# Sink logits as an extra score column, and VectorE's high/low splits spread over the steps of an attention loop

## What is computed

```python
s = jnp.einsum('bqkgd,bskd->bkgqs', qb, kb, preferred_element_type=jnp.float32) * scale
s = jnp.where(mask, s, NEG_INF)
sink = jnp.broadcast_to(sinks.reshape(KV, G)[None, :, :, None, None], s.shape[:-1] + (1,))
p = jax.nn.softmax(jnp.concatenate([s, sink], axis=-1), axis=-1)[..., :-1]
...
return (o * jax.nn.silu(gate)) @ w_out
```

## Time and profile before

| what | value |
|---|---|
| runs | 2717.4, 2725.14, 2715.82 us (median 2717.4) |
| the profiled execution | 2716.97 us, of which the span is 2715.2 us |
| PE busy | 2407.9 us, 89% |
| DVE busy | 1598.5 us, 59% |
| POOL busy | 915.3 us, 34% |
| ACT busy | 765.6 us, 28% |
| mean granted PE clock | 0.921 of full |

### The profile page before, as it was taken

The page is one execution under the profiler, slowest core; times in us unless marked ns, Lnnn a source line. Parts: engine busy times, 40 slices in busy tenths (PEclk is TensorE's granted clock), DMA queues, the critical chain, the costliest instruction groups (busy, mean ns, idle before and its releaser), DMA issues.

```text
span 2715.2 us, 31261 instructions
## 1 busy us (share of the span) xinstructions
PE 2407.9 (89%) x12233; PEld 1833.5 (68%) x12233; DVE 1598.5 (59%) x2435; ACT 765.6 (28%) x1706; POOL 915.3 (34%) x944
## 2 busy tenths in 40 slices
PE   3969898788999899799969989999998997999988
PEld 2756676567987666677747776577677685757666
DVE  7786674763235566664664557674745445958373
ACT  2233202512001355224331233221402215232231
POOL 2873897387800345781120010401302001040030
PEclk6979898798678899899989999999999999999999
DMA  6440455044543100441011211121121121213111
GB/s 213 140 132 8 117 135 129 1 116 117 127 78 62 32 1 3 123 116 63 32 58 59 71 48 63 32 78 63 47 93 63 62 63 33 62 47 93 47 62 62
DMA packets 229157, 200.27 MB, mean 74 GB/s; under 512 B 86835, under 2 KB 213139, under 8 KB 228755
## 3 DMA queue, kind: packets, MB, share of 16 engines
q1 hardware_dynamic: 217491, 156.33, 20.6%
q0 software_dynamic: 11520, 41.95, 5.2%
HBM read 196.16 MB, written 2.10 MB: 73 GB/s over the span
## 4 chain that ended last, share of the span: by engine, by line
PE 57%; POOL 17%; DVE 17%; ACT 5%; issue 3%; DMA 0%; SPq 0%; DVEq 0%; ACTq 0%; POOLq 0%
PE bank L506 13%; PE bank L507 13%; PE bank L508 13%; POOL mix L2220 6%; POOL mix L2217 4%; PE bank L618 4%; DVE wring_parts L1515 3%; PE bank L654 3%; POOL mix L2223 2%; PE bank L632 2%; POOL mix L2204 2%; DVE whi_parts L1514 2%; PE bank L818 2%; DVE qb L1959 1%; PE bank L572 1%
## 5 line engine op out<-in xcount | busy, mean ns | idle before, releaser
L507 PE MATMUL bank<-h_parts,whi_parts 128*128 128x512 f32 (+2 forms) x1336 | 539.5, 404 | 0.0
L1515 DVE TENSOR_TENSOR wring_parts<-wring,whi_parts 128x2048 fp32r<-128x2048 f32 (+1 forms) x138 | 326.4, 2365 | 4.7
L1514 DVE CAST whi_parts<-wring 128x2048 fp32r<-128x2048 f32 (+1 forms) x138 | 192.3, 1394 | 201.5 <-PE bank L508 167.1
L507 PEld LDWEIGHTS bank<-h_parts,whi_parts 128*128 128x128 f32 (+2 forms) x1336 | 253.6, 190 | 69.2 <-issue 5.9
L2220 POOL TENSOR_TENSOR mix<-mix 128x512 f32<-128x512 f32 (+1 forms) x160 | 214.5, 1341 | 12.5
L506 PE MATMUL bank<-vt_parts,whi_parts 128*128 128x512 f32 (+2 forms) x472 | 199.9, 424 | 18.1 <-POOL h_parts L2251 12.1
L507 PE MATMUL bank<-mix_parts,whi_parts 128*128 128x512 f32 x512 | 202.9, 396 | 0.0
L506 PE MATMUL bank<-pt_parts,whi_parts 128*128 128x512 f32 x392 | 166.3, 424 | 36.7 <-DVE wring_parts L1515 20.9
L508 PE MATMUL bank<-vt_parts,wring_parts 128*128 128x512 f32 (+2 forms) x472 | 190.4, 403 | 0.0
L1586 DVE CUSTOM_DVE_ANT_0 bank<-bank,causal 128x128 f32<-128x128 f32 (+3 forms) x256 | 120.2, 512 | 76.0 <-PE bank L618 75.6
L618 PE MATMUL bank<-kb,qb 64*128 64x128 f32 (+3 forms) x1024 | 156.7, 385 | 8.7 <-ACT pr L1199 4.0
(11 more groups left out here) (375 smaller groups left out, 5363.9 us busy)
## 6 DMA issues: line engine op xcount, KB each, us to landing
wring<-in_w_in SPq DMA_DIRECT2D x60, 1024.0 KB, 5.2
mix<-in_ada_w POOLq DMA_DIRECT2D x80, 512.0 KB, 4.6
wring<-in_w_out SPq DMA_DIRECT2D x16, 1024.0 KB, 5.1
wring<-in_mla_w_in SPq DMA_DIRECT2D x10, 1024.0 KB, 7.0
wring<-in_mla_w_out SPq DMA_DIRECT2D x8, 1024.0 KB, 5.2
wring<-in_swa_w_in SPq DMA_DIRECT2D x32, 256.0 KB, 4.7
wring<-in_nsa_w_in SPq DMA_DIRECT2D x32, 256.0 KB, 4.5
wring<-in_nsa_w_in SPq DMA_DIRECT2D x6, 1024.0 KB, 5.2
```

The costliest lines, as they stand in the source:

```text
L507: pe.matmul(bank, lh, rl, start=False, stop=False)
L1514: chain(dve.tensor_copy(high, whole))
L1515: dve.tensor_tensor(low, whole, high.bitcast(F32), ALU.subtract).then_inc(done, 1)
```

## The change

Two edits. First, in L = 1 PE writes the sink of each head as one more column behind the scores, by a matmul of one row of ones (128 columns) with one element of the sink, so that ACT's exponential over n+1 columns sums it too; ACT's 128x1 exponentials and DVE's addition go. Second, `split` is taken apart in the attention loops of all layers: the gate scaling of a unit's output stays at its step, the high cuts follow one step later and the low cuts two steps later; the high cut of a weight unit stays at steps 5 and 9, its low cut moves to steps 7 and 11. In MLA the two high cuts of a unit stand together, and so do the two low cuts. After the last step all three stages follow one another. `prepare` and `split` outside these loops are as before.

```diff
@@ PE, attention, score(m)
+                    if L == 1:
+                        for s in range(2):
+                            row, e = slice(s * HD, s * HD + 1), sink_of(u, s)
+                            pe.matmul(b[s][:, n:n + 1], ones[row, :], sink[row, e:e + 1], start=True, stop=True)
@@ ACT, attention, exps(m)
-                        if L == 1:
-                            e = sink_of(u, s)
-                            act.activation(stat_at(3, m, s), sink[:, e:e + 1], ACT.Exp, scale=-1.0, bias=stat_at(0, m, s))
-                        act.activation(rows_slot(m, s)[:, 0:n], bank[:, 0:n], ACT.Exp, scale=-1.0, bias=stat_at(0, m, s),
+                        wide = n + 1 if L == 1 else n
+                        act.activation(rows_slot(m, s)[:, 0:wide], bank[:, 0:wide], ACT.Exp, scale=-1.0, bias=stat_at(0, m, s),
                                        accum_out=stat_at(1, m, s)).then_inc(SC.empty, 1)
@@ DVE
+            def part_high(whole, high):
+                dve.tensor_copy(high, whole).then_inc(own_step, 1)
+                cut[0] = cnt(own_step)
+            def part_low(whole, low, high, done):
+                dve.wait_ge(*cut[0])
+                dve.tensor_tensor(low, whole, high.bitcast(F32), ALU.subtract).then_inc(done, 1)
+            def prepare_high():
...
+                dve.wait_ge(w_loaded[n % W_SLOTS], landed[n])
+                if s >= HI_SLOTS:
+                    dve.wait_ge(*unit_done[split_units[s - HI_SLOTS]])
+                part_high(part(W[n % W_SLOTS]), part(W_HIGH[s % HI_SLOTS]))
+            def prepare_low():
...
+                part_low(part(W[n % W_SLOTS]), part(W_LOW[n % W_SLOTS]), part(W_HIGH[s % HI_SLOTS]), w_split)
@@ DVE, attention
                 def row_sum(m):
                     dve.wait_ge(*SC.emptied((L, "s", m, 1)))
-                    if L == 1:
-                        chain(dve.tensor_tensor(stat_pair(1, m), stat_pair(1, m), stat_pair(3, m), ALU.add))
                     dve.reciprocal(stat_pair(2, m), stat_pair(1, m)).then_inc(rinv_ready, 1)
...
-                    if u and i == (0 if L in (0, 3) else 1):
-                        out_unit(u - 1)
+                    stage = m % NT - (0 if L in (0, 3) else 1)
+                    if u and 0 <= stage < 3:
+                        out_unit(u - 1, stage)
                     if m in PREPARE_AT:
-                        prepare()
-                out_unit(pairs(L) - 1)
+                        prepare_high()
+                    if m - 2 in PREPARE_AT:
+                        prepare_low()
+                for stage in range(3):
+                    out_unit(pairs(L) - 1, stage)
```

More of the change, by code:

```diff
@@ L1774, in _, with out_unit @@
                         late_constants()
-                    def out_unit(u):
+                    def out_unit(u, stage):
                         for e in (2 * u, 2 * u + 1):
[L1778 to L1783, removed]
+                            if stage == 0:
+                                dve.wait_ge(*O.filled((L, "o", e)))
+                                dve.scalar_tensor_tensor(out=mix[:, e, :], in0=O.take((L, "o", e))[:, :], scalar=0.5, in1=mix[:, e, :],
+                                                         op0=ALU.mult, op1=ALU.mult).then_inc(O.empty, 1)
+                            elif stage == 1:
+                                dve.wait_ge(*O.emptied((L, "o", e)))
+                                part_high(mix[:, e, :], mix_high(L)[e])
+                            else:
+                                part_low(mix[:, e, :], mix_parts[:, e, :], mix_high(L)[e], mix_split)
                 elif kind == "swa":
@@ L1794, in _, with out_unit @@
                             prepare()
[L1796 to L1801, removed]
+                    def out_unit(g, stage):
+                        if stage == 0:
+                            dve.wait_ge(*O.filled((L, "o", g)))
+                            dve.scalar_tensor_tensor(out=mix[:, g, :], in0=O.take((L, "o", g))[:, :], scalar=0.5, in1=mix[:, g, :],
+                                                     op0=ALU.mult, op1=ALU.mult).then_inc(O.empty, 1)
+                        elif stage == 1:
+                            dve.wait_ge(*O.emptied((L, "o", g)))
+                            part_high(mix[:, g, :], mix_high(L)[g])
+                        else:
+                            part_low(mix[:, g, :], mix_parts[:, g, :], mix_high(L)[g], mix_split)
                 else:
@@ L1866, in _, with out_unit @@
                         dve.tensor_copy(ex[:, :, i * P:(i + 1) * P], V.take((L, "tc", i))[:, :].rearrange("p (g n) -> p g n", g=4)).then_inc(V.empty, 1)
-                    def out_unit(u):
-                        if u % 2:
-                            b = u // 2
+                    def out_unit(u, stage):
+                        b = u // 2
+                        if u % 2 == 0:
+                            return
+                        if stage == 0:
                             dve.wait_ge(*O.filled((L, "o", b)))
@@ L1947, in _ @@
                     gate((L, "gate", 4 + b), mix[:, 4 + b, :])
-                attention(L, lambda u: head_copy("do", u))
+                attention(L, lambda u, stage: head_copy("do", u) if stage == 0 else None)
                 head_out("do", 4, DIFF_H, lambda e: col("diff_norm_w_2", l), 0.5 * (1.0 - LAM_INIT[l]))
```

13 lines of the change are left out of this document (12 added, 1 removed).

## The result

The changed kernel takes 2678.9 us (median of 4 executions, 2677.4 to 2680.3) against 2717.5 us before, a ratio of 0.986 with a 95% interval of 0.984 to 0.987. The forecast was 2676 us.

A forecast was written before the change was run, and what follows sets the result against it. PE works nearly all the time but stalls where long DVE cuts precede short operations others need. Savings of 5.2 + 4.0 + 14.1 + 6.6 + 10.8 = 40.7 us from 2716.97 give 2676 us; forecast 2669 to 2681, range 2659 to 2699.

The forecast's parts named there:

- L = 4 and 5: Attention of layers 4 and 5: relieving step 9 of its splits saves 3.3 us each, 6.6 us.
- L = 1: Attention of layer 1: sink column and separated splits make it PE bound, 8.4 us a unit, saving 10.8 us.
- 6.6 + 4 x 0.35 = 8.0, with 0.4 us of gaps 8.4: Steady unit of L = 1: 6.6 us PE work, four steps of sink matmuls at 0.35 us, gaps: 8.4 us.
- 3 us for stretches in which the clock still falls: L = 1, six units: 3 us added for clock falls after the weight cuts DVE cannot hide.
- 4.2 us: L = 1, steps 5 to 7 and 9 to 11: 4.2 us added because DVE cannot hide the weight cuts.
- L = 2: Attention of layer 2: output and weight cuts moved away, fewer slow groups, less 1.0 us for moved low cuts: 14.1 us saved.
- a sign of being wrong: Next profile: the forecast is wrong if low cuts of steps 7 and 11 have waiters on POOL; no size given.
- L = 0 and 3: MLA attention layers: with the weights' low cut off step 5, stalls shrink, saving 5.2 us and 4.0 us.
- 0.3 us: MLA units: stall of 0.3 us left per unit, because cover for the moved low cut is thin for its first follower.
- Rival (c): L = 1: PE stays at its lower clock throughout, 16.8 us a unit, slower, about 2724 us in total; chance 0.05.
- (a): L = 1: sink matmuls cost their upper bound, 0.63 us a step; about 1 us gained there, total 2686 us; chance 0.25.
- (b): Moved low cuts stall at their new places, 2.29 us for each of ten, total about 2699 us; chance 0.08.

The follow-up runs named there:

- e8: The changed kernel once more, unaltered: 2681.0 us (6 executions, five from 2674.6 to 2681.6 and one of 2711.1).
- e3: The changed kernel with the output's low cuts one step later in the MLA layers, beside the weights' low cut: 2704.1 us.
- e7: The changed kernel with a test behind its end, POOL scaling tiles beside five kinds of DVE work: 2712.2 us, test included.
- e12: The changed kernel with the sink column copied by DVE instead of sink matmuls, and the MLA output's low cuts one step later: 2668.2 us.
- e4: The changed kernel with, in the MLA layers, the output's low cuts one step earlier and the weights' high cut one step later: 2711.3 us.
- e5: The changed kernel with the weights' low cuts of L = 2 one step later, at steps 8 and 12: 2685.5 us.
- e10: The changed kernel without the sink edit, and with the MLA output's low cuts one step later: 2679.5 us.
- e2: The kernel before with the sink edit alone, every split left whole: 2732.4 us, 1.006 of before.
- e11: The kernel of e4 once more, unaltered: 2686.2 us (12 executions, eight from 2679.4 to 2690.5, four from 2712.1 to 2715.7).

## Why the prediction was right, and which terms were not

The total came within 3 us of 2676. The mechanism forecast is seen: low cuts away from the reciprocals, and a PE-bound L = 1. That the number is so near is in part luck, twice over. The terms miss in both directions: 4.5 us too little in L = 1, and 3.2, 1.2 and 2.7 us too much in L = 2, 0 and 3. And the four executions all had the high course, which neither e8 nor the kernels next to it always have. Of the two edits the splits carry the total, as far as the totals tell: e1, without the sink edit, takes 2678.0 us. Term by term:

- **L = 4 and 5**, 6.6 us forecast, 3.6 + 3.0 measured; 0.7 us of L = 4 hang on the clock, by e3, e7 and e12 (40.4 us at 0.79, where the kernel before had 0.80).
- **L = 1**, 10.8 us forecast, 15.3 measured. The sink price of 0.35 us a step was 0.31. The unit of "6.6 + 4 x 0.35 = 8.0, with 0.4 us of gaps 8.4" was 7.88: there are no gaps, 0.5 us for each of six units. The "3 us for stretches in which the clock still falls" did not come: from 482 us on the clock is 1.00. With 3.1 us for the units and these 3 us the term is 17, 1.6 over what was measured; where these 1.6 us went no run shows. The waits of PE at the two weight units, 0.92, 0.93, 1.17 and 0.93 us from 482 to 498 us, come near to the "4.2 us" forecast for them. By e1, 10.3 us of it come from the splits and 5.0 from the sink edit.
- **L = 2**, 14.1 us forecast, 10.9 measured. The cuts were right; the clock at the stage's start was not thought of. In its first two windows of 12 us the changed kernel had 0.56 and 0.87, the kernel before 0.71 and 1.00. e4, with 0.71 and 1.00 as before, took 14.5 us less than before; e1 had 1.00 in the whole stage and took 16.3 us less. The size of this term moves by 5 us with that start. The prediction also named a sign of being wrong, low cuts of steps 7 and 11 with waiters on POOL, and it came: two scalings of 128x128, 0.88 us in e5, are held to 2.99 and 3.42 us in the changed kernel. But here the cover held, and PE waits 0.23 and 0.66 us for them, 0.9 us in all where the forecast had 1.0 for the moved low cuts. In MLA the same pair takes 2.90 us at step 7 (at 1256.02), and PE doesn't wait for it at all.

```profile
910.54 2.99 POOL pr L2291 x2
921.74 3.42 POOL pr L2291 x2
913.57 0.44 PE L636 MATMUL bank<-ident,pr 128*128 128x128 f32 x2 [0.23 <-POOL pr L2291]
925.20 0.44 PE L636 MATMUL bank<-ident,pr 128*128 128x128 f32 x2 [0.66 <-POOL pr L2291]
```

- **L = 0 and 3**, 5.2 and 4.0 us forecast, 4.0 and 1.3 measured. The step that failed is the stall of "0.3 us" a unit: "step 6 two low cuts" was costed at nothing beyond DVE's queue. They shut POOL out of the second scaling, 1.05 us a unit, and PE waits 1.48 us for that one; with the cuts elsewhere, in e10, it waits 0.42. e3's edit gives back 2.2 us in L = 0, and in e10 2.1 us in L = 3. A third hold stands at the last step of both layers: the low cuts of the unit before have nothing behind them on DVE there, the last scaling takes 1.72 us, and PE waits 1.87 us for it (1.86 in L = 3) where it waited 0.73 before. e3 and e10 don't remove it (1.87 us in both), nor does e12, the best kernel.
- **Rival (c)**, the slower one, had a chance of 0.05 and 2724 us. It is real, with 2711 us and a unit of 13.8 us instead of 16.8. Its "6.6 x 1.8 = 11.8" was right (13.81 - 4 x 0.52 = 11.7 us); its 1.26 us for the new matmuls was more than twice too high. Its chance was set too low, by an argument that fell: that PE would have its full clock "here it would work more". In the low course it works 8.00 of 8.00 us and keeps 1.2 GHz for 100 us. The row that spoke for the rival, 0.50 with PE busy without pause, was before me. Forecast and rival are two courses of one kernel, and the chance of each is no property of the code that these runs settle. In e2 it came in 5 of 6 executions, which makes the sink edit by itself a loss.
- **Rivals (a) and (b)** fell: 0.31 us a step and not 0.63, and the longest stalls of PE behind a moved low cut are 1.87 us in MLA, at the last step, and 0.66 us in L = 2, not 2.29.

## What to carry to other kernels

A long operation moved to a quiet place in its own queue must also be quiet for its neighbour: on this chip a DVE subtraction with both operands in SBUF, or an SBUF-to-SBUF cast, stopped GpSimd's scaling of a tile in SBUF for its whole length and was itself held by one under way, while DVE work with an operand in PSUM did neither (e7). Small matmuls put on TensorE to spare other engines can cost more through the clock (33 us in L = 1) than through their length (32 pairs of 0.31 us); run such a kernel some ten times before its median is believed, and compare stages by windows with the granted clock beside them. Where a narrow operation is wanted, ask each engine for it: 64 copies of 128x1 on DVE did what 64 matmuls (128 records in the trace) did, for 3.4 us less in L = 1, and the low course was not seen in five executions.

## What the runs showed of the hardware that was not expected

- TensorE at 1.2 GHz, busy 8.00 of 8.00 us in the windows quoted of e3, stayed there nearly to the end of the stage of 107.81 us (mean clock 0.51). The Trainium skill, "TensorE: Matmul & The Clock Gate", section Part 1: The HAM clock gate, says that activity releases the throttle; PE's busy time as the profile shows it did not go with a release here. In e4 the clock rose at 477 us after 16 us of the same work; in e11, the same kernel, it did not.
- GpSimd's 128x512 scaling: 0.77 us alone, 2.88 us when it met one 128x2048 subtraction, 1.81 us with a cast of that size. The subtraction takes 2.29 us, and 2.75 when it began beside a scaling under way.
- A one-row, one-column matmul pair costs 0.31 us in line at 2.4 GHz and 0.52 at 1.2 GHz; a second pair behind it 0.43 at 1.2 GHz; with 64 rows the scores behind the pair are 0.10 us shorter at 1.2 GHz.
- A 128x1 copy from SBUF to PSUM takes DVE 0.14 to 0.21 us.
